# The last down projection of an encoder layer: half 0 finished first, its scatter between the two row blocks of half 1

## The reference

```python
y = jnp.zeros_like(t)
for e in range(N_EXPERTS):                      # 16
    h = jax.nn.silu(t @ w1[e]) * (t @ w3[e])    # w1, w3: 1024 x 512
    y = y + combine[:, e:e + 1] * (h @ w2[e])   # w2: 512 x 1024
x = x + y
```

## Time and profile before

| | |
|---|---|
| median of three runs | 637.66 us (637.64 to 637.67) |
| the profiled execution | 638.16 us |
| its span, first to last instruction | 636.3 us |
| mean granted TensorE clock | 0.998 |
| TensorE busy | 621.9 us, 98% |
| VectorE, ScalarE, GpSimd busy | 180.1, 139.4, 53.3 us |
| chain that ended last | TensorE 93%, VectorE 3%, ScalarE 2% |
| down projections (L1460), passes | 960, 593 ns each, overlapped |

### The profile page before, as it was taken

One profiled execution on the slowest core, in us unless ns is written; L12 is line 12 of the kernel. 1 busy time (PEld: TensorE's weight loads), 2 busy tenths in 40 slices (PEclk: granted clock), 3 DMA queues, 4 the chain that ended last, 5 costly groups with the idle time before them and its releaser, 6 DMA issues.

```text
span 636.3 us, 10482 instructions
## 1 busy us (share of the span) xinstructions
PE 621.9 (98%) x4409; PEld 256.6 (40%) x4409; DVE 180.1 (28%) x608; ACT 139.4 (22%) x372; POOL 53.3 (8%) x61
## 2 busy tenths in 40 slices
PE   9999999999999999999999999999999999999996
PEld 6445544434324334333244455443343343343221
DVE  1665834512102102100133767353021021021011
ACT  2136642210000000000131677331100000000011
POOL 0005420000000000000010475000000000000000
PEclk9999999999999999999999999999999999999999
DMA  8999909699999999999999997596999999999993
GB/s 318 292 274 422 376 2 369 230 408 418 421 420 422 420 420 420 422 420 420 398 295 252 365 403 250 221 388 249 423 420 421 421 420 421 420 421 420 421 416 115
DMA packets 44759, 229.94 MB, mean 361 GB/s; under 512 B 8271, under 2 KB 8561, under 8 KB 21666
## 3 DMA queue, kind: packets, MB, share of 16 engines
q1 hardware_dynamic: 43068, 224.66, 90.4%
q0 software_dynamic: 1312, 4.23, 2.0%
q10 hardware_dynamic: 326, 0.31, 0.2%
HBM read 228.10 MB, written 1.08 MB: 360 GB/s over the span
## 4 chain that ended last, share of the span: by engine, by line
PE 93%; DVE 3%; ACT 2%; issue 1%; POOL 0%; DVEq 0%; ACTq 0%
PE ps L1448 35%; PE ps L1460 18%; PE ps L1210 12%; PE ps L1297 8%; PE ps L1409 5%; PE ps L1417 3%; PE ps L1279 2%; PE ps L1245 2%; PE ps L1266 2%; ACT attw L572 1%; PE ps L1524 1%; PE ps L1430 1%; PE ps L1164 1%; PE ps L1150 1%; PE ps L1158 1%
## 5 line engine op out<-in xcount | busy, mean ns | idle before, releaser
L1448 PE MATMUL ps<-attw,work 128*32 128x512 f32 x1216 | 140.1, 593 | 0.0
L1460 PE MATMUL ps<-ring,work 128*32 128x512 f32 x960 | 105.0, 593 | 0.5 <-ACT work L648 0.5
L1448 PE MATMUL ps<-ring,work 128*32 128x512 f32 x832 | 100.5, 594 | 0.0
L1210 PE MATMUL ps<-attw,work 128*128 128x512 f32 x192 | 87.4, 598 | 0.3 <-DVE work L760 0.3
L1448 PEld LDWEIGHTS ps<-attw,work 128*32 128x32 f32 x1216 | 40.1, 110 | 89.1 <-issue 89.1
L1297 PE MATMUL ps<-attw,work 128*128 128x512 f32 x128 | 60.1, 603 | 0.7 <-issue 0.5
L1460 PEld LDWEIGHTS ps<-ring,work 128*32 128x32 f32 x960 | 30.3, 110 | 70.0 <-issue 68.3
L1017 DVE TENSOR_TENSOR work<-work,ps 128x256 f32<-128x256 f32 (+1 forms) x24 | 11.5, 508 | 156.1 <-PE ps L1448 156.1
L1448 PEld LDWEIGHTS ps<-ring,work 128*32 128x32 f32 x832 | 27.3, 110 | 57.7 <-issue 53.0
L1210 PEld LDWEIGHTS ps<-attw,work 128*128 128x128 f32 x192 | 34.6, 190 | 38.2 <-issue 37.4
L440 POOL TENSOR_SCALAR attw<-attw,stat 128x256 f32<-128x256 f32 x40 | 40.8, 1024 | 51.6 <-DVE stat L878 51.4
(11 more groups left out here) (161 smaller groups left out, 463.6 us busy)
## 6 DMA issues: line engine op xcount, KB each, us to landing
ring<-in_w_dram SPq DMA_DIRECT2D x112, 1024.0 KB, 26.0
attw<-in_w_dram SPq DMA_DIRECT2D x80, 1024.0 KB, 19.3
attw<-in_w_qkv_dram SPq DMA_DIRECT2D x4, 2048.0 KB, 17.6
attw<-in_w_o_dram SPq DMA_DIRECT2D x8, 1024.0 KB, 22.6
attw<-in_w_qkv_dram SPq DMA_DIRECT2D x8, 512.0 KB, 11.2
ring<-bias_rows POOLq DMA_DIRECT2D x16, 256.0 KB, 7.0
x_sb<-in_x_dram SPq DMA_DIRECT2D x2, 512.0 KB, 6.8
out_dram<-x_sb SPq DMA_DIRECT2D x2, 512.0 KB, 4.5
```

What stands on the lines that cost most here:

```text
L1210: last = pe.matmul(ps[:, g, :], xT[:, k, P * tt:P * tt + P], wqkv[part][:, k, :], start=(k == 0), stop=(k == KB - 1))
L1448: last = pe.matmul(ps[row:row + SLOTS, bank[t], :], xg[:, k, t, row:row + SLOTS], w[:, e, k % 4, :], start=(k == 0), stop=(k == KB - 1), t ...
L1460: last = pe.matmul(ps[row:row + SLOTS, bank[t], :], hT[t][:, k, row:row + SLOTS], w[:, e, k % 2, 512 * half:512 * half + 512], start=(k == ...
```

## The change

For the last unit of the last group (p = 1, kh = 1) of each layer, four row blocks are left: half 0 and half 1, each with the hidden blocks k = 2 and k = 3. Before, their order was (half 0, k 2), (half 1, k 2), (half 0, k 3), (half 1, k 3), scatter of half 0, scatter of half 1. Now it is (half 0, k 2), (half 0, k 3), (half 1, k 2), scatter of half 0, (half 1, k 3), scatter of half 1. The wait for `last_half_landed` moves one row block up. `scatter_pair` gets a list of halves. The pair p = 0, the first three groups, and the extra rounds keep their order.

```diff
-                def scatter_pair(m, R, p, final):
-
-                    for half in range(2):
+                def scatter_pair(m, R, p, final, halves):
+
+                    for half in halves:
...
-                    if p:
+                    if p and 1 in halves:
                         last.then_inc(m.scattered, 1)
...
                             if final and p and kh and not fetch:
-                                for half in range(2):
-                                    down(g, p, kh, half, unit, [0])
+                                down(g, p, kh, 0, unit, [0])
                                 pe.wait_ge(last_half_landed, 16 * (R + 1))
-                                for half in range(2):
-                                    down(g, p, kh, half, unit, [1]).then_inc(m.w2_used, 1)
+                                down(g, p, kh, 0, unit, [1]).then_inc(m.w2_used, 1)
+                                down(g, p, kh, 1, unit, [0])
+                                scatter_pair(m, R, p, final, [0])
+                                down(g, p, kh, 1, unit, [1]).then_inc(m.w2_used, 1)
                                 continue
...
                         if not fetch:
-                            scatter_pair(m, R, p, final)
+                            scatter_pair(m, R, p, final, [1] if final and p else range(2))
```

## The result

The changed kernel takes 640.05 us (median of 6 runs, 639.60 to 640.59) against 637.65 us for the kernel before in the same comparison (637.27 to 637.77): a ratio of 1.0036 with a 95% interval of 1.0026 to 1.0046. That is 2.40 us slower, where 2.46 was forecast. The profiled execution took 639.60 us with a span of 637.8.

A forecast was written before the change was run, and what follows sets the result against it. TensorE, busy for 98% of the span, was taken as the bound. Each layer pays 1.23 us, so 2 x 1.23 = +2.46 us on the median 637.66 gives 640.1 us, range 638.9 to 641.0.

The forecast's parts named there:

- The price of a layer: End of each layer: last row block and copy of half 1 come 1.23 us later (0.14 + 0.97 + 0.12).
- scatter and switch: TensorE, ahead of (half 1, k 3): scatter of half 0 takes 0.97 us, return to a row block 0.12, including 0.09.
- Rival 1: Layer 1 catches up the delay of layer 0, so only the end of layer 1 counts: 638.9 us; chance 0.08.
- Rival 2: On TensorE's array the last row block passes or streams beside the waiting scatter: 637.7 us, same; chance 0.04.
- rival 3: More than a shift: last weights land after their new wait in layer 0, or clock or branch costs extra: 641.8 us; chance 0.08.
- the 0.8 us that the prediction had left for it: Layer 0: last weights land at 313.0, new wait at 313.83, so 0.8 us are left and the moved wait costs zero.
- The copy-outs: VectorE's L1130 waits for the flag load behind half 1's copy, not half 0's scatter, so it moves by 1.23 us.
- The end: Kernel end: second store is issued after L1133 and lands 4.7 us later, last thing of the kernel; price +1.23 us.
- Rival 4: Faster: half 0's earlier store leaves alone; the second store's 4.7 us must shrink by more than 2.46 + 1.3; chance 0.02.

The follow-up runs named there:

- the run above: The new order of row blocks with only TensorE's flag load moved ahead of the last group, against the kernel before: 639.45 against 637.84 us, ratio 1.0027.

## Why the prediction was right

**The price of a layer.** 1.23 us was worked out, and the positions say 1.23 and 1.22. The parts came out as well: from the start of half 0's copy to its scatter 0.75 us (314.27 to 315.02), as in the kernel before; and scatter and switch (315.02 to 316.08 is 1.06; 0.97 + 0.09 had been taken from the earlier trace rows). The run without the scatter between shows that this is all of the cost, and the run with the scatter at once shows that the same grid also forecasts a third order (9.23 us expected, 9.22 measured). The total agrees better than it can be measured: the interval of the result is 1.7 to 2.9 us, and the two single layers sum to 2.1, so that 2.40 stands so near to 2.46 is partly luck.

**Two layers, nothing absorbed.** Rival 1 is refuted by the layers taken singly and by the distance of 302.3 to 302.7 us through layer 1. Each layer alone is about as large as what can just be told from no change, so the positions in the trace bear more of this than the two medians. Rival 2, the looser order, is refuted by the wait of 0.82 us ahead of a scatter with work behind it.

**Nothing extra.** Of rival 3, the last weights were in time in the changed kernel: the seven row blocks of pair 1 run as one piece of 6.21 and 6.22 us. But the 0.8 us that the prediction had left for it were taken from one landing of 26.2 us; with the 27.0 of the run above they were used up, and TensorE stalled by 0.14 us in all. That is one of the eight profiled executions that have the new wait in layer 0; in the other seven the row blocks show no stall. The clock stayed at its upper level, 2.4 GHz: in this stretch of the changed kernel (length, busy of five engines, PEclk, DMA share, GB/s) TensorE waits 0.82 us ahead of the last scatter, and PEclk is 1.00.

```profile
629.50:631.00 1.50, 0.68 (x10) 0.13 (x4) 0.69 (x1) 0.58 (x1) 0.00 (x0) 1.00 0.00 0
```

**The copy-outs.** That L1130 hangs on the flag load and not on the scatter was right for the changed kernel (1.48 and 1.19 us behind the copy, forecast 1.49 and 1.20). For the kernel before, the prediction said that the scatter had no part in it. That was too strong: with the load out of the way, only 0.44 us in layer 0 and 0.15 in layer 1 were won before the scatter held it. It made no difference for the sum.

**The end.** The prediction let the second store land a fixed 4.7 us behind its issue. The issue moved by 1.7 us on the clock of these two executions (631.1 to 632.8), or 2.4 with the 0.70 us by which the changed kernel's had started earlier. The landing was 4.6, but over all runs the two stores landed between 3.5 and 5.1 us behind their issue, with TensorE's flag load as one cause. This term was treated as constant on the strength of one row; it held here, since both kernels have that load at the same place. That it held to 0.1 us between two single executions is luck as well: with the load in that place the end behind the issue still varied from 4.7 to 5.5 us. Rival 4, faster through the stores, would have needed 3.8 us from here, more than the end of the kernel varied in any run.

## What to carry to other kernels

Between two engines that hand work to and fro, put independent work of the first where the second works. Here the scatter of half 0 had covered the copy of half 1; moved ahead of the row block on which that copy waits, it covers nothing, and its whole 1 us goes into the chain, although half 0 was done earlier. Finishing something earlier is worth nothing if what uses it stands in program order behind something that became later.

Look at what stands behind the last real work of an engine. A flag whose value has been fixed for long was loaded at the end here. By the positions that cost 0.4 us between the layers, which the medians don't confirm, and by the medians about 0.8 at the end of the program. The three kernels with the flag early and no scatter between the row blocks came out 0.62, 0.77 and 0.78 us under the kernel before. The noise doesn't tell these three apart, and only of the last (with the order "half 0, half 1, both scatters", which by itself made no difference) does the whole interval lie below 1: 0.04 to 0.22%.

## What the runs showed of the hardware beyond that

The time of the first work varies from execution to execution by more than most effects here: the first projection began at 6.81 and 7.51 us in two executions with the same instructions up to there. The time from the issue of the second store to the end of the span was 4.1 to 5.5 us, and 4.1 to 4.5 in all five runs in which TensorE has no flag load behind its last matmul.

The list of waits named the scatter (L1430) as what VectorE's L1130 waited for in the kernel before (0.50 us), while in the changed one the same gap of 0.50 us is put down to issue. The flag load ended last in both, before by only 0.15 us. A gap whose length does not change when what the list names for it has moved by a microsecond is worth a run in which the other candidate is taken away.
